# MoE stages: rows for the experts gathered by 0/1 matrices on TensorE instead of through x_rows in memory, with a shorter routing and weight pieces released singly

## What is computed

```python
g_w, g_idx = lax.top_k(jax.nn.softmax(g_logits, axis=-1), 1)      # 4 groups
e_w, e_idx = lax.top_k(jax.nn.softmax(e_logits, axis=-1), 2)      # 2 of 8 experts in the group
h = jax.nn.silu(xb @ w_gate[e]) * (xb @ w_up[e]);  y_rows = h @ w_down[e]
x = _layer_norm_2(DEEPNORM_ALPHA_2 * x + ffn, ln_g[i, 1], ln_b[i, 1])
```

## Time and profile before

| | us |
|---|---|
| median of three runs | 4502.24 |
| lowest and highest run | 4499.92, 4510.23 |
| span of the profiled execution, first to last instruction | 4483.4 |
| first load of layer 0's MoE to the start of its experts | 2720.8 to 2767.0 |
| experts of layer 0, first to last Silu | 2781.7 to 3298.3 |
| first load of layer 1's MoE to the start of its experts | 3805.1 to 3853.1 |
| experts of layer 1, first to last Silu | 3869.1 to 4421.4 |

### The profile page before, as it was taken

How to read it: one execution, slowest core, us unless ns; L and a number is a source line. 1 busy time by engine, 2 the same in 40 slices (tenths; PEclk the granted TensorE clock), 3 DMA queues, 4 the chain that set the end, 5 groups by cost and what they waited for, 6 DMA issues and landing times. The chain is left out here.

```text
span 4483.4 us, 62137 instructions
## 1 busy us (share of the span) xinstructions
PE 3907.5 (87%) x25636; PEld 2697.6 (60%) x25636; DVE 1702.6 (38%) x3092; ACT 701.0 (16%) x1502; POOL 831.2 (19%) x667
## 2 busy tenths in 40 slices
PE   7999989999999889999999996877749998677774
PEld 3578876784447777874448844444429976344442
DVE  6657757630465655221440613000033254200003
ACT  2212111110222221010211511000020033000000
POOL 1122214430110314420100202000013343100001
PEclk8999999999999999999999997989979999799997
DMA  3221313632121011232122025999962200899995
GB/s 134 66 95 49 124 44 131 219 129 99 48 66 57 2 53 59 92 108 66 49 75 68 1 85 223 398 400 402 401 237 67 85 1 34 329 401 394 404 401 227
DMA packets 253162, 708.80 MB, mean 158 GB/s; under 512 B 22441, under 2 KB 136689, under 8 KB 202253
## 3 DMA queue, kind: packets, MB, share of 16 engines
q1 hardware_dynamic: 234378, 660.87, 39.9%
q10 hardware_dynamic: 13956, 28.00, 1.7%
q0 software_dynamic: 4608, 16.78, 0.9%
HBM read 668.35 MB, written 37.24 MB: 157 GB/s over the span
## 5 line engine op out<-in xcount | busy, mean ns | idle before, releaser
L3374 PE MATMUL experts_pg<-moe_wg,experts_xt 128*64 128x256 f32 x4224 | 522.1, 410 | 132.8 <-DMA moe_wg<-in_moe_w_up 113.6
L3374 PEld LDWEIGHTS experts_pg<-moe_wg,experts_xt 128*64 128x64 f32 x4224 | 330.0, 148 | 307.9 <-issue 155.8
L3389 PE MATMUL experts_py<-moe_wd,experts_ht 128*64 128x512 f32 x1056 | 259.8, 636 | 41.6 <-DVE experts_ht L3444 24.1
L629 PE MATMUL ffn_out_y<-ffn_out_ring,ffn_h 128*128 128x512 f32 x640 | 275.9, 592 | 0.0
L3442 DVE TENSOR_TENSOR experts_h<-experts_hs,experts_pg 128x256 f32<-128x256 f32 x66 | 27.8, 421 | 642.4 <-ACT experts_hs L3408 642.4
L714 PE MATMUL ffn_in_seven<-ffn_in_seven_t,ffn_in_seven_s 128*128 128x256 f32 x1056 | 237.6, 381 | 1.7 <-DVE ffn_in_seven_t L787 0.8
L3474 POOL DMA_INDIRECT merge_yg<-y_rows,moe_yi x16 | 16.1, 1007 | 1103.8 <-PEq L3461 568.2
L714 PEld LDWEIGHTS ffn_in_seven<-ffn_in_seven_t,ffn_in_seven_s 128*128 128x128 f32 x1056 | 201.1, 191 | 31.6 <-DVE ffn_in_seven_t L787 1.6
L629 PEld LDWEIGHTS ffn_out_y<-ffn_out_ring,ffn_h 128*128 128x128 f32 x640 | 121.1, 190 | 151.6 <-issue 150.2
L3389 PEld LDWEIGHTS experts_py<-moe_wd,experts_ht 128*64 128x64 f32 x1056 | 82.7, 144 | 173.1 <-issue 173.1
L3438 DVE COPY experts_xt<-experts_px 128x512 f32<-128x512 f32 x66 | 45.6, 692 | 332.0 <-PE experts_px L3366 332.0
(11 more groups left out here) (755 smaller groups left out, 6814.9 us busy)
## 6 DMA issues: line engine op xcount, KB each, us to landing
moe_wg<-in_moe_w_gate SPq DMA_DIRECT2D x66, 2048.0 KB, 20.2
moe_wg<-in_moe_w_up SPq DMA_DIRECT2D x66, 2048.0 KB, 24.7
moe_wd<-in_moe_w_down SPq DMA_DIRECT2D x66, 2048.0 KB, 25.5
ffn_in_ring<-in_ffn_w_in SPq DMA_DIRECT2D x42, 1024.0 KB, 5.3
ffn_in_ada_ring<-in_ada_w SPq DMA_DIRECT2D x28, 1024.0 KB, 6.9
ffn_out_ring<-in_ffn_w_out SPq DMA_DIRECT2D x20, 1024.0 KB, 5.3
ssd_proj_ring<-in_ssd_w_in SPq DMA_DIRECT2D x19, 1024.0 KB, 5.4
att_kqt<-in_attn_w_qkv SPq DMA_DIRECT2D x17, 1024.0 KB, 5.1
```

The costliest lines, as they stand in the source:

```text
L629: last = nc.tensor.matmul(y[:, tt, half, :], h[:, kk, tt * P:(tt + 1) * P], ring[n][:, q, half * BANK:(half + 1) * BANK], start=(kk == 0), ...
L3374: last = nc.tensor.matmul(pg[ch * SLOTS:(ch + 1) * SLOTS, b, side, 0:HH], xt[:, b, kk % MQ, kk // MQ, :], wg[:, b, side, kk, ch * HH:(ch + ...
L3389: last = nc.tensor.matmul(py[half * SLOTS:(half + 1) * SLOTS, b, :], ht[:, b, kk % HM, kk // HM, :], wd[:, b, kk, half * HALF:(half + 1) * ...
```

## The change

`x_rows` and all that served it go: the scatters, the loads of `xg`, the list's places `xi` and the zeroing of its tail in an early stage. In the experts stage DVE compares, for a pair of blocks, the slot numbers of all assignments (`yf`, lowered by 128 from pair to pair) with a row 0..127 (`seat`) and adds both choices: `sel`, a 0/1 matrix of tokens by slots. A unit is four product calls, one for each token tile, with 128 columns of x (taken with a stride of four) as the stationary operand and `sel` as the moving one: it makes an eighth of the gathered and transposed rows for both blocks at once. The units of the next pair stand between the steps of this one: two before a block's gate product, one after up, one after the transposes of h. Fifteen pairs are written out with constants, and only the last regular pair and those beyond are in a loop. Gate, up and down have a semaphore each, are waited for singly and are refilled singly. The table `info` moves behind the first gather and is smaller. `py` has one buffer instead of two, `px` two banks instead of one. In the routing the steps by token tile become single operations, and two product calls do the counting, with the sums over tiles on DVE. x is no longer multiplied by ALPHA: the gates are divided by it and the merge's norm uses a smaller epsilon.

```diff
-        self.plain = False
+        self.plain, self.eps = False, LN_EPS
...
-        nc.vector.tensor_scalar(self.root[:, tt:tt + 1], self.mv[:, tt, 1:2], LN_EPS, None, ALU.add).then_inc(self.var_done, 1)
+        nc.vector.tensor_scalar(self.root[:, tt:tt + 1], self.mv[:, tt, 1:2], self.eps, None, ALU.add).then_inc(self.var_done, 1)
...
-                     for r_ in (k.x_rows[l][ASSIGN:, :], k.y_rows[l][FIRST * SLOTS:, :])
+                     for r_ in (k.y_rows[l][FIRST * SLOTS:, :],) for r in range(0, r_.shape[0], P) for h in range(D // BANK)]
...
+        def load_gate(sp, e, w):
+            sp.dma_start(halves(gate_up(w, 0)), w_gate[:, e, :, :]).then_inc(gate_in[w], 16)
+        def load_up(sp, e, w):
+            sp.dma_start(halves(gate_up(w, 1)), w_up[:, e, :, :]).then_inc(up_in[w], 16)
+        def load_down(sp, e, w):
+            sp.dma_start(halves(down(w)), w_down[:, e, :, :]).then_inc(down_in[w], 16)
...
-                    accumulate(nc, pct[:, :], [(k.ones[:, :], m[:, q, :]) for q in range(TT)]).then_inc(s["counted"], 1)
+                    nc.tensor.matmul(pct[:, :, :], k.ones[:, :], m[:, :, :], start=True, stop=True).then_inc(s["counted"], 1)
+                    nc.tensor.matmul(prk[:, :, :], k.causal[:, 0, :], m[:, :, :], start=True, stop=True).then_inc(s["counted"], 1)
...
+                    step(V.tensor_scalar(limit[:, :], io[:, 0:ROUNDS], float(SLOTS), None, ALU.mult))
+                    step(V.tensor_scalar(early[:, :], io[:, :], float(SLOTS), None, ALU.mult))
+                    step(V.memset(before[:, 0, :], 0.0))
...
+                    le = lg[:, :, G:].rearrange("p t (g e) -> p t g e", g=G)
+                    in_group = ohg[:, :, :].unsqueeze(3).to_broadcast([P, TT, G, PER])
+                    step(V.tensor_tensor(big[:, :, :, :], le, in_group, ALU.mult))
+                    step(V.tensor_reduce(es[:, :, :], big[:, :, :, :].rearrange("p t g e -> p t e g"), AX.X, ALU.add))
...
+                        step(V.tensor_tensor(mj[:, j, :, :].rearrange("p t (g e) -> p t g e", g=G), in_group,
+                                             oh[j][:, :, :].unsqueeze(2).to_broadcast([P, TT, G, PER]), ALU.mult))
+                    V.tensor_tensor(m[:, :, :], mj[:, 0, :, :], mj[:, 1, :, :], ALU.add).then_inc(s["m_done"], 1)
...
+                    step(V.tensor_scalar(tmp[:, :], ew[:, :], 1.0, ALPHA, ALU.add, ALU.mult))
...
                     dve.wait_ge(s["counted"], 1)
+                    for tt in range(1, TT):
+                        step(V.tensor_tensor(before[:, tt, :], before[:, tt - 1, :], pct[:, tt - 1, :], ALU.add))
+                    step(V.tensor_tensor(cnt[:, :], before[:, TT - 1, :], pct[:, TT - 1, :], ALU.add))
+                    dve.wait_ge(s["counted"], 2)
+                    step(V.tensor_tensor(rank[:, :, :], before[:, :, :], prk[:, :, :], ALU.add))
...
+                    step(V.tensor_scalar(late[:, :, :], rank[:, :, :], float(SLOTS), None, ALU.is_ge))
...
+                    step(V.tensor_tensor(pos[:, :, :], rank[:, :, :], late[:, :, :], ALU.add))
+                    for j in range(2):
+                        step(V.tensor_tensor(picked[:, j, :, :], pos[:, :, :], mj[:, j, :, :], ALU.mult))
+                    step(V.tensor_reduce(yf[:, :, :], picked[:, :, :, :], AX.X, ALU.add))
...
+            QUARTER = DK // 2
...
+            hit, sel = st.sb("hit", [P, 2, TT, P]), st.sb("sel", [P, 2, TT, P])
+            xt = st.sb("xt", [P, 2, DK, P])
+            yb = st.sb("yb", [P, 2, HALF])
...
+                    def load(n, e, w, before):
+                        sp.wait_ge(s["gate_made"], before + 1)
+                        load_gate(sp, e, w)
+                        sp.wait_ge(s["gu_made"], before + 1)
+                        load_up(sp, e, w)
+                        sp.wait_ge(s["y_made"], before + 1)
+                        load_down(sp, e, w)
+                    for n in range(2, 2 * LAST):
+                        load(n, one_of(n), slot(n)[0], n - 2)
+                    end = pairs_end(sp)
+                    with sp.Fori(LAST, end) as it:
                         for b in range(2):
-                            load(2 * it + b, b)
+                            n = 2 * it + b
+                            e = sp.value_load(info[0:1, bass.ds(n, 1)], min_val=0, max_val=E - 1)
+                            load(n, bass.ds(e, 1), slot(2 * LAST + b)[0], n - 2)
...
+                    def unit(p, kk):
+                        q = p % 2
+                        for tt in range(TT):
+                            at = (kk // 4) * HALF + kk % 4
+                            last = nc.tensor.matmul(px[:, kk, :], k.x[:, tt, at:(kk // 4 + 1) * HALF:4], sel[:, q, tt, :],
+                                                    start=(tt == 0), stop=(tt == TT - 1))
+                        if kk % QUARTER == QUARTER - 1:
+                            last.then_inc(s["xt_made"], 1)
...
+                    def begin(p, half):
+                        if p:
+                            pe.wait_ge(s["xt_taken"], 2 * p + half - 1)
+                        if half == 0:
+                            pe.wait_ge(s["sel_done"], p + 1)
...
+                    def one(n, b, q, w, use, between=None, first=False):
...
+                            pe.wait_ge((gate_in, up_in)[side][w], 16 * use + 16)
...
+                            last.then_inc(s[("gate_made", "gu_made")[side]], 1)
+                        if between is not None:
+                            unit(between, b * QUARTER + 2)
...
+                        if between is not None:
+                            unit(between, b * QUARTER + 3)
...
+                        pe.wait_ge(down_in[w], 16 * use + 16)
                         if not first:
...
+                            pe.wait_ge(s["y_taken"], n)
...
+                    for half in range(2):
+                        begin(0, half)
+                        for kk in range(half * QUARTER, (half + 1) * QUARTER):
+                            unit(0, kk)
+                    for p in range(LAST):
+                        after = p + 1 if p + 1 < LAST else None
                         for b in range(2):
-                            one(2 * it + b, b, it)
+                            n = 2 * p + b
+                            if after is not None:
+                                begin(after, b)
+                                unit(after, b * QUARTER)
+                                unit(after, b * QUARTER + 1)
+                            if b == 0:
+                                pe.wait_ge(s["xt_taken"], 2 * p + 2)
+                            one(n, b, p % 2, *slot(n), after, n == 0)
+                    end = pairs_end(pe)
+                    with pe.Fori(LAST, end) as it:
+                        for half in range(2):
+                            pe.wait_ge(s["xt_taken"], 2 * it + half - 1)
+                            if half == 0:
+                                pe.wait_ge(s["sel_done"], it + 1)
+                            for kk in range(half * QUARTER, (half + 1) * QUARTER):
+                                unit(LAST, kk)
+                        pe.wait_ge(s["xt_taken"], 2 * it + 2)
+                        for b in range(2):
+                            w, use = slot(2 * LAST + b)
+                            one(2 * it + b, b, LAST % 2, w, it - LAST + use)
...
+                        act.wait_ge(s["gate_made"], n + 1)
...
+                    nc.gpsimd.iota(seat[:, :], pattern=[[1, P]], base=0, channel_multiplier=0,
+                                   allow_small_or_imprecise_dtypes=True).then_inc(s["seat_done"], 1)
...
+                    def select(p, q, first=False):
+
+                        if not first:
+                            dve.wait_ge(s["moved"], p)
+                            dve.wait_ge(s["sel_done"], p)
+                        V.tensor_tensor(hit[:, :, :, :], yf[:, :, :].unsqueeze(3).to_broadcast([P, 2, TT, P]),
+                                        seat[:, :].rearrange("p (j t n) -> p j t n", j=1, t=1).to_broadcast([P, 2, TT, P]),
+                                        ALU.is_equal).then_inc(s["hit_done"], 1)
+                        dve.wait_ge(s["hit_done"], p + 1)
+                        V.tensor_tensor(sel[:, q, :, :], hit[:, 0, :, :], hit[:, 1, :, :], ALU.add).then_inc(s["sel_done"], 1)
+                        V.tensor_scalar(yf[:, :, :], yf[:, :, :], -float(P), None, ALU.add).then_inc(s["moved"], 1)
+
+                    def take(p, half, q):
+                        dve.wait_ge(s["xt_made"], 2 * p + half + 1)
+                        V.tensor_copy(xt[:, q, half * QUARTER:(half + 1) * QUARTER, :], px[:, half * QUARTER:(half + 1) * QUARTER, :]).then_inc(s["xt_taken"], 1)
...
+                        dve.wait_ge(s["gu_made"], n + 1)
+                        V.tensor_tensor(h[:, b, :], hs[:, b, :], pg[:, b, 1, 0:HH], ALU.mult).then_inc(s["h_done"], 1)
...
```

(32 more changed lines are left out.)

256 lines of the change are left out of this document (84 added, 172 removed).

## The result

The changed kernel takes **4594.23 us** (median; 4591.07 to 4597.65). The ratio to the kernel before is 1.0208, with a 95% interval of 1.0189 to 1.0226: slower by about 2%, clear of no change, where 4381 was forecast. Of the four runs of the kernel before beside it one took 7839.38 us and is left out of the comparison. The changed kernel's profiled execution has a span of 4589.3 us.

What follows compares the result with a forecast made beforehand. DMA was taken to bound the expert stages, with TensorE second and not far away. First refills 2 x 18.0, blocks 77.5 and ends 2 x 4 sum to 121.5 us; 4502.2 less that is 4380.7, range 4360 to 4435.

Steps and rivals of the forecast that it cites:

- part 2: First block of an expert stage: a unit costs 0.96 us, the first refill comes 18.3 us after the experts' start.
- rival A: Expert blocks: TensorE becomes the bound at a clock of 0.90, 16.3 us a block, time 4416; chance 0.17.
- The routing, 21.5: Routing ahead of the experts: fewer, larger operations and two counting calls let the experts open 21.5 us earlier.
- The first block, 18.3 from the experts' start to the first refill: Start of the expert stage: sel, ten units and the gate product take 18.3 us, 3.5 more than before.
- First refill 18.0 earlier: Start of each layer's expert stage: 21.5 saved in routing less 3.5 lost in the first block; bounds 20.3 and 9.3.
- A block at 15.8, bound by DMA, 1.25 less: Expert blocks: without x rows' loads, weights 14.92 and y stores 0.77 remain; 62 x 1.25 = 77.5 us saved.
- Rival B: Expert blocks: small packets cost only what their bytes cost, 0.66 us a block, time 4417; chance 0.12.
- TensorE's block at 14.4: Expert blocks: TensorE's new work, four units included, takes 14.4 us at full clock, staying under the transfers' 15.8.
- The tail, 4 a layer: End of each expert stage: TensorE ends 4 to 6 us behind down's last weights; 4 saved, between 0 and 5.
- The sum, 121.5: Whole kernel: first refills 2 x 18.0, blocks 77.5 and ends 2 x 4 save 121.5 us, giving 4380.7.
- 18.8 us "around the span": Whole kernel: the median 4502.24 exceeds the span 4483.4 by 18.8 us, which lies around the span and stays.
- Rival C: Expert stages: fetching fifteen written-out pairs' code stalls TensorE, slower than before, 4604 at 5 us a stall; chance 0.04.

Runs made afterwards that it cites:

- the copy: Changed kernel with ACT copying x once a layer into a tile where a unit's columns lie side by side: 4364.24 us, ratio to before 0.9702.

## Why the prediction was wrong

**The step that failed** is in part 2: "The stationary operand is read with a stride of four numbers, as the old transposes read theirs, whose loads take 212 ns and are no multiple of the pace; I take 0.12 between records." The 212 ns was taken to "not show a doubling", but the prediction names no load without a stride beside it. Against the 190 to 193 of ordinary fp32 product loads in other stages of before it is a tenth more; a transpose's load without a stride takes 140. Like against like, the stride costs a factor of 1.5, and a product's load of 192 would have become some 290; it became 329, and the distance between records 0.235 where neighbouring numbers have 0.113. A unit costs 1.88 us, not 0.96. The rest of the miss follows from this one number: four units a block are 3.9 us more than with neighbouring numbers, TensorE's block goes from under the transfers' to 18.72, and the first refill, with ten units ahead of it, comes 7.7 us later.

The prediction had this outcome in words, with the unit at "some 1.9 us and TensorE the bound", from the page that speaks against the read, and called it rival A in a harsher form. But it gave it no time and no chance. Worked out, it is 14.4 + 32 x 0.115 = 18.1 a block, so 62 x 1.05 = 65 slower, less 17 at the starts, where ten doubled units take 9.4 of each 18.0, and plus 7 at the ends, where eight uncovered ones take 7.7 against the 4 saved: about 4555, an estimate, on the other side of no change and outside the range. The 4416 of rival A priced a slow clock, not a doubled read.

**Point by point**, by the copy's kernel, in which only this number is put right:

- *The routing, 21.5.* It gave 22.0 in layer 0. Right.
- *The first block, 18.3 from the experts' start to the first refill.* 17.3 in the copy, 25.1 in the changed kernel. The ten units took 11.13 us in the copy; 7.7 + 1.9 and a loss of 2.3 to the clock were forecast, 11.9. *First refill 18.0 earlier:* 19.4 and 22.5 in the copy's two layers, 11.7 in layer 0 of the change.
- *A block at 15.8, bound by DMA, 1.25 less.* Late in the stage a block takes 15.5 in the copy, 1.55 less. From the first refill to the landing of the last down weights the copy takes 474.5 and 505.5 us where before takes 514.7 and 548.8: 83.5 less, which is 1.35 for each of 62 blocks. Part of the gap between the two figures is the end of the copy's transfers, which ran at 233 and 271 GB/s from 3238 to 3242 us; the rest is not taken apart. The loads alone are worth 1.44 to 1.5, at or above the upper bound of 1.43: the y stores were charged 0.77 by their packets and cost what their bytes cost, and for the x rows it is the reverse, 1.5 us for 0.26 MB. Rival B, 0.66 a block, is refuted with this.
- *TensorE's block at 14.4.* 14.84 with neighbouring numbers: the y_taken wait and DVE were rightly nothing, and the missing 0.44 is not taken apart here.
- *The tail, 4 a layer.* Too much. The copy's TensorE ends 5.2 and 7.9 us behind the landing of the last down weights, near the 4 to 6 of the forecast, but before ended only 7.5 and 8.9 behind it, and not 10: 2.3 and 1.0 are saved. The single pieces are worth their price (the pairing put back costs 3.9 at the end of layer 0), and the loop's uncovered gather takes part of it back.
- *POOL's scaling, the zeroing and the epsilon at nothing:* no run speaks for another price, and none tests them singly.
- *The sum, 121.5.* The copy's medians differ by 130.9. From a layer's first load to the end of its last down product it takes 521.3 and 555.0 us, before 583.2 and 621.9: 128.8 less. The first refills give 42.0 of it (36 forecast), the blocks 83.5 (77.5), the ends 3.3 (8). So the mechanism held, and no term but the stride's was off by more than 6 us. The spans differ by 121.2 only, since the copy's profiled execution reached the MoE 8.3 us later, by the scatter told above; that this equals the sum is luck.
- *18.8 us "around the span".* Wrong: the runs list a span beside each time, and it is 1.7 to 2.1 us shorter. The profiled execution of before, then, was quicker than any of the three runs beside it. The sum wasn't hurt, since it was taken off the median.
- *Rival C, code.* Not at all: in the copy, with the same written-out pairs, the first 20 Silus or so keep a step of 14.84 us to the hundredth.
- *Rival A, by the clock.* The opposite: a TensorE that never waits is granted 1.00 from 2900 to 3000 us.

## What to carry to other kernels

Before a matmul operand is read with a stride, look for the pace with and without it in rows of the same kind of instruction: a load that hides behind a wait shows its price in its duration alone. With fp32 numbers side by side or two to 16 bytes the read ran at full pace here (0.113 and 0.120 us a record), with each in 16 bytes of its own it took twice as long (0.235 and 0.240), and one strided copy on an idle engine buys the pace back for all the reads that follow. And when a second bound is 10% away, a rival that doubles one of its terms needs its own number and its own chance, above all if a written rule names it.

## What was not expected of the hardware

- The stride costs on either operand: 329 ns instead of 192 for the load, 405 instead of 275 for the product.
- It costs more in a product's load (192 to 329 ns) than in a transpose's (140 to 212). No run tells why.
- The 64-row loads of x in 128 KB pieces cost 1.44 to 1.5 us of full DMA a block for 0.26 MB, the y stores of the same size only their bytes, 0.6 us at 421 GB/s.
- Releasing weights earlier, singly, lowered the rate from 401 to 388 GB/s where these loads were in the traffic (before against the same with single pieces), and not where they were gone (421 in the copy with either).
